# Retention in four chunks of 256 tokens, and the LRU gates' half-empty products in row-group pairs, in a one-core float32 decoder trunk

## The chip, the cores and the metric

One core of a Trainium2 chip (trn2) runs the whole program. The metric is the device time of one execution in microseconds. A product is made of matrix instructions on TensorE (PE in the rows); VectorE is DVE, ScalarE is ACT, GpSimd is POOL, and SyncE (SP) issues the weight DMAs. PEld are the loads of the stationary operand of a matrix instruction.

## What is computed

Two layers on 1024 tokens of width 1024, each a token mixer and a SwiGLU feed-forward. Layer 0 mixes by retention, layer 1 by a gated linear recurrence (RG-LRU). The parts that the change touches:

```python
# retention, 4 heads, dk = 256, dv = 512, state carried over chunks
scores = einsum(q_i, k_i) * intra
o = scores @ v_i + (q_i @ state) * q_decay
state = state * chunk_decay + (k_i * k_decay).T @ v_i
o = rms_norm(o) * silu(g)
# RG-LRU, width 1536, gates are block diagonal: 8 blocks of 192
r = sigmoid(einsum('bsnc,ncd->bsnd', u, w_r) + b_r)
i = sigmoid(einsum('bsnc,ncd->bsnd', u, w_i) + b_i)
a = exp(-8 * softplus(-lam) * r)
b = sqrt(1 - a**2) * (i * u)
h_t = a_t * h_{t-1} + b_t ; y = h * gelu(gate) ; out = y @ w_out
```

The chunk length is free: the sum is the same for any.

## The kernel before

Every product is float32 made of three products of rounded operands (helper `three`, lines 773, 776 and 777: upper by upper, upper by lower, lower by upper), each 128 rows by 128 columns of stationary operand and up to 512 moving columns. An upper part is an ACT or POOL copy, a lower part a DVE or POOL subtraction. PSUM has 8 banks of 512 columns. Jobs that fill a bank are numbered; `psum_full` and `psum_free` count them in order, and `free(e)` lets TensorE wait until job e-8, the earlier user of the bank, is freed.

**Retention.** `head(h)` runs four times. On TensorE: q and k (`tile_rows`), G (the gate, 8 banks), the scores, the turning of k (products with an identity, lines 966 and 967), V (8 banks), then `values(s)` for the eight blocks of 128 tokens, `o_turns` (transposes, line 1009) and the output product. The scores are taken for two chunks of 512 tokens (`CHUNK = 4`): each chunk has key blocks that meet 512, 384, 256 and 128 queries. The state is summed once (`state_sum`, from the first chunk), rounded (ACT line 1500, DVE line 2060), and used by the four blocks of the second. DVE masks the scores (line 2038), splits them (line 2043) and the turned k (line 2048). ACT squares each output block (line 1495) and takes the root (line 1505); DVE gates it (line 2065) and scales it (line 2073). Ahead of that, DVE turns q and k by position (lines 2000 to 2021), first both halves of q, then of k.

**LRU.** The width is cut into four groups of three tiles of 128 (`GT = 3`, items 0 to 5 are three tiles by two halves of 512 tokens). Group by group TensorE does: u (`lru_into(..., 0)`, three times 48 products), the gate branch (`lru_into(..., 6)`), the output product of the group before (`lru_outof`), and then the r and i gates (`lru_gates`). Gate blocks are 192 wide, tiles 128: tile 0 meets rows of tiles 0 and 1, tile 1 those of all three, tile 2 those of 1 and 2 (`MEETS`), so 7 products of three instructions for each of r and i and each half; for the pairs (0, 1) and (2, 1) only 64 of the 128 rows hold anything.

The gate chain follows from the banks: ACT does the sigmoids (lines 1768 and 1773), DVE multiplies u by i and frees two banks (`gated`, line 2392), ACT does tanh, exp and square root (1782, 1786, 1792), each after a load of its function table; DVE does lines 2400 and 2404, the scan (2409) and the gating (2416); ACT rounds y (1800) and DVE splits it (2421). Items go in pairs (0, 1), (2, 3), (4, 5). In DVE's order the next group's convolution (`conv`, lines 2365 and 2367) stands behind the last line 2421 of this group. It reads u's banks, and tile 1 of the next gate branch reuses the first two of them. POOL meanwhile splits the weights of the coming products (touch line 560, cast line 569, subtraction line 571; for the gates' weights 732 and 734).

The last group differs: its gates stand in the midst of the output product of the third. Blocks 0 to 3 come ahead of them, then 4 to 7 (whose banks are those of items 2 and 3), and then the second half (banks of items 4 and 5).

Of the kernel before, what the change touches and what calls it, by code (L numbers as in the profile page):

```python
# [14 lines left out]
P = 128  # L15
D = 1024
S = 1024
# [19 lines left out]
CHUNK = 4  # L37

SCORES = [pieces for c in (0, CHUNK) for pieces in ([(c, 512)], [(c + 3, 128), (c + 1, 384)], [(c + 2, 256)])]
MASK_AT = (P, 0, P)  # L40
SCORE_N = [sum(n for _, n in pieces) for pieces in SCORES]
KT_AT = sum(SCORE_N[:3])
SCORE_AT = [sum(SCORE_N[:i]) + (2 * 512 if i >= 3 else 0) for i in range(len(SCORES))]

KEYS_AT = {c: SCORE_AT[i] + sum(n for _, n in pieces[:j])
           for i, pieces in enumerate(SCORES) for j, (c, _) in enumerate(pieces)}
STATE_AT = sum(SCORE_N) + 2 * 512
SCORE_COLS = STATE_AT + 2 * 512

OT_AT = (0, SCORE_AT[3])  # L50

MEETS = [(0, 1), (0, 1, 2), (1, 2)]
# [4 lines left out]
J_QK, J_G, J_S, J_K, J_V, J_O, J_T, J_W = 0, 8, 16, 22, 24, 32, 40, 48  # L57
# [3 lines left out]
def o_job(s):  # L61

    return J_O + s + (4 if s == SB - 1 else 0)


def t_job(s):
    return J_O + s + (SB - 1 if s < 4 else SB)
# [101 lines left out]
def build(nc, x, positions, mix_norm, ffn_norm, final_norm, ret_w_in, ret_w_out, lru_w_in, lru_conv_w,  # L169
# [3 lines left out]
    with ctx:  # L173
# [79 lines left out]
        def k_turned(d):  # L253

            c = slice(KT_AT + d * 512, KT_AT + (d + 1) * 512)
            return b_hi[:, c], b_lo[:, c]
# [117 lines left out]
        mask_in, k_rounded = sem("mask_in"), sem("k_rounded")  # L374
        st_full, st_rounded, st_ready = sem("st_full"), sem("st_rounded"), sem("st_ready")
# [391 lines left out]
        def _(pe):  # L767
# [164 lines left out]
            def head(h, first, last=False):  # L932
# [11 lines left out]
                for i, pieces in enumerate(SCORES):  # L944
                    if i == 0:
                        pe.wait_ge(qk_ready, h * 8 + 8)
                    free(base + J_S + i)
                    at = 0
                    for c, n in pieces:

                        hf, q = c // CHUNK, c % CHUNK * P
                        for d in range(2):
                            (k_h, k_l), (q_h, q_l) = qk_at(1, d, hf), qk_at(0, d, hf)
                            m = three(bank(J_S + i, at, n), k_h[:, q:q + P], k_l[:, q:q + P],
                                      q_h[:, q:q + n], q_l[:, q:q + n], d == 0, d == 1)
                        at += n
                    m.then_inc(psum_full, 1)
# [3 lines left out]
                for d in range(2):  # L961
                    free(base + J_K + d)
                    k_h, k_l = qk_at(1, d, 0)
                    for c in range(CHUNK):
                        cut, o = slice(c * P, (c + 1) * P), bank(J_K + d, c * P, P)
                        nc.tensor.matmul(o, k_h[:, cut], ident_r[:], start=True, stop=False)
                        m = nc.tensor.matmul(o, k_l[:, cut], ident_r[:], start=False, stop=True)
                    m.then_inc(psum_full, 1)
# [4 lines left out]
                def state_sum():  # L973

                    pe.wait_ge(psum_free, base + J_V + SB)
                    for d in range(2):
                        k_h, k_l = k_turned(d)
                        for c in range(CHUNK):
                            cut, v = slice(c * P, (c + 1) * P), slice(c * 512, (c + 1) * 512)
                            m = three(bank(J_O + 6 + d), k_h[:, cut], k_l[:, cut], a_hi[:, v], a_lo[:, v],  # L980
                                      c == 0, c == CHUNK - 1)
                        m.then_inc(st_full, 1)

                pe.wait_ge(s_ready, h * len(SCORES) + len(SCORES))
                def values(s):
                    late = s >= CHUNK
                    pe.wait_ge(psum_free, base + J_V + s + 1)
                    if s >= 6:

                        pe.wait_ge(st_ready, 2 * h + s - 6 + 1)  # L990
                    for c in range(CHUNK if late else 0, s + 1):
# [3 lines left out]
                                  c % CHUNK == 0, not late and c == s)  # L995
                    for d in range(2 if late else 0):
                        if s == CHUNK:
                            pe.wait_ge(st_ready, 2 * h + d + 1)
                        (q_h, q_l), (st_h, st_l), at = qk_at(0, d, 1), state(d), (s - CHUNK) * P
                        m = three(bank(J_O + s), q_h[:, at:at + P], q_l[:, at:at + P], st_h, st_l, False, d == 1)  # L1000
# [12 lines left out]
                for s in range(3):  # L1013
                    values(s)
                state_sum()
                for s in range(3, SB - 1):
                    values(s)
                o_turns(range(4))
                values(SB - 1)
# [237 lines left out]
            def lru_gates(g, base, e0, u_hi, u_lo):  # L1257

                pe.wait_ge(wri_ready, 2 * g + 2)
                for hf in range(2):  # L1260
                    for tile in range(GT):
                        for m_i in range(2):
                            e = e0 + (hf * GT + tile) * 2 + m_i
                            free(base + e)
                            if m_i == 0 and (hf, tile) in ((0, 0), (0, 1), (1, 1)):

                                pe.wait_ge(u_ready, len(U_PIECES) * g + 2 + tile + hf)
                            for kt in MEETS[tile]:
                                w = slice(m_i * 1152 + kt * 384 + tile * P, m_i * 1152 + kt * 384 + (tile + 1) * P)
                                r = slice(kt * S + hf * 512, kt * S + (hf + 1) * 512)  # L1270
                                m = three(bank(e), wri_hi[:, w], wri_lo[:, w], u_hi[:, r], u_lo[:, r],
                                          kt == MEETS[tile][0], kt == MEETS[tile][-1])
                            m.then_inc(psum_full, 1)

            def lru_outof(g, u0, base, e0, nh, y_hi, y_lo):
                for k in range(GT):
                    j = nh * 3 + k
                    if nh == 0:
                        pe.wait_ge(y_ready, g * 6 + k + 4)
# [18 lines left out]
            for first in (0, 4):  # L1298
                for k in range(GT):
                    if first == 0:  # L1300
                        pe.wait_ge(y_ready, (GROUPS - 2) * 6 + k + 4)
                        pe.wait_ge(w_ready, u0 + 12 + k + 1)
                    w = slice(k * 512, (k + 1) * 512)
                    for s in range(first, first + 4):
                        e = (L_OUT if first == 0 else L_OUT_LAST - 4) + s
                        if k == 0:
# [3 lines left out]
                                  k == 0, k == GT - 1, s == (4 if k else 0))  # L1310
# [10 lines left out]
            def y_there(half, k, i):  # L1321
                if i == 0:
                    pe.wait_ge(y_ready, (GROUPS - 1) * 6 + half * GT + k + 1)
# [12 lines left out]
        def _(act):  # L1336
# [114 lines left out]
            def head(h, first):  # L1451
# [7 lines left out]
                for i in range(8):  # L1459
                    pair, hf, d = i // 4, (i // 2) % 2, i % 2  # L1460
                    act.wait_ge(rope_out, h * 8 + i + 1)
                    nc.scalar.activation(qk_at(pair, d, hf)[0], (t(0), t(1), t(2), r3(7))[i % 4], ACT.Copy)\
                        .then_inc(qk_rounded, 1)
# [7 lines left out]
                for i, n in enumerate(SCORE_N):  # L1471
                    act.wait_ge(psum_free, base + J_S + i + 1)
                    nc.scalar.activation(b_hi[:, SCORE_AT[i]:SCORE_AT[i] + n], T[:, (i % 3) * 512:(i % 3) * 512 + n],
                                         ACT.Copy).then_inc(s_rounded, 1)
                for d in range(2):
                    full(base + J_K + d)
                    nc.scalar.activation(k_turned(d)[0], bank(J_K + d), ACT.Copy).then_inc(k_rounded, 1)
# [5 lines left out]
                act.wait_ge(s_ready, h * len(SCORES) + len(SCORES))  # L1483
# [7 lines left out]
                for s in range(SB):  # L1491
# [5 lines left out]
                    if s == 2:  # L1497
                        for d in range(2):
                            act.wait_ge(st_full, 2 * h + d + 1)
                            nc.scalar.activation(state(d)[0], bank(J_O + 6 + d), ACT.Copy).then_inc(st_rounded, 1)  # L1500
                    if s == 6:
                        o_turned_upper(range(4))
                    if s % 4 == 3:
                        act.wait_ge(o_sq, h * 8 + s + 1)
                        nc.scalar.activation(rstd[:, s - 3:s + 1], ssq[:, s - 3:s + 1], ACT.Sqrt, bias=eps,
                                             scale=1.0 / DV).then_inc(o_root, 1)
                o_turned_upper(range(4, SB))
# [253 lines left out]
            def gate_chain(g, base, e0, y_hi):  # L1761
                def gates(i):

                    tile = i % GT
# [11 lines left out]
                def tanh_exp(items):  # L1776

                    for i in items:
                        if i >= 2:
# [3 lines left out]
                                             scale=gc_gate[:, 21 + i % GT:22 + i % GT]).then_inc(r_tanh, 1)  # L1783
                    for i in items:
                        act.wait_ge(r_tanh, 6 * g + i + 1)
                        nc.scalar.activation(r_buf[i % 4], r_buf[i % 4], ACT.Exp,
                                             scale=gc_gate[:, i % GT:i % GT + 1]).then_inc(a_exp, 1)
# [6 lines left out]
                def y_round(items):  # L1794
                    for i in items:
# [3 lines left out]
                        at = i % GT * S + i // GT * 512  # L1799
# [5 lines left out]
                gates(1)  # L1805
                tanh_exp((0, 1))
                roots((0, 1))
                gates(2)
# [51 lines left out]
        def _(dve):  # L1860
# [130 lines left out]
            def head(h, last=False):  # L1991
                base = JB_RET + h * HEAD_JOBS
                dve.wait_ge(rope_in, h * 32 + 32)
                for pair in range(2):
# [22 lines left out]
                    for i in range(4):  # L2017
# [4 lines left out]
                            .then_inc(qk_ready, 1)  # L2022
                    dve.wait_ge(qk_ready, n + 4)
                dve.wait_ge(rope_saved, 32)
# [5 lines left out]
                for i in range(len(SCORES) + 1):  # L2030
                    if i < len(SCORES):
                        n, m = SCORE_N[i], MASK_AT[i % 3]
                        if i >= 3:
                            dve.wait_ge(s_ready, h * len(SCORES) + i - 2)
                        else:
                            dve.wait_ge(psum_free, base + J_S)
                        full(base + J_S + i)
                        TT(T[:, (i % 3) * 512:(i % 3) * 512 + n], bank(J_S + i, 0, n), dk[:, m:m + n], ALU.mult)\
                            .then_inc(psum_free, 1)
                    if i:  # L2040
                        n, a = SCORE_N[i - 1], SCORE_AT[i - 1]
                        dve.wait_ge(s_rounded, h * len(SCORES) + i)
# [491 lines left out]
```

## Time and profile before

| | us |
|---|---|
| median of 3 runs (2706.28 to 2706.48) | 2706.4 |
| the profiled execution | 2707.8 |
| its span, first to last instruction | 2706.0 |
| TensorE busy | 2673.6 |
| TensorE's loads of the stationary operand | 2213.3 |
| VectorE busy | 1272.0 |
| ScalarE busy | 830.3 |
| GpSimd busy | 1266.6 |

1.8 us of the profiled execution lie outside its span. A row of a timeline gives the start, the duration, engine, line, operation and operands; the next instruction of an engine may start before the duration of the last is over, since they are pipelined: a 512-column instruction lasts 0.39 us, and they start 0.227 us apart. The idle time ahead of an instruction, and who ended it, stands in brackets.

### The profile page before, as it was taken

The page shows a single profiled execution, that of the slowest core. Times are in us where ns is not written, and L with a number is a line of the kernel's source. Part 1 is how long each engine was busy: PE and PEld are TensorE (multiplying, and loading weights), DVE is VectorE, ACT ScalarE, POOL GpSimd, SP SyncE. Part 2 cuts the span into 40 slices and gives each one's busy share as a digit, 9 for nine tenths or more (in the row PEclk, how much of TensorE's full clock was granted, in tenths as well). Part 3 has the DMA queues.
Part 4 walks back from the last instruction along what each step waited for, and adds up shares of the span by engine and source line. Part 5 has one row for each costly group of instructions (what it writes and reads, how often), then busy time and mean ns, then how long its engine had stood idle before and what let it go on. Part 6 is the DMA issues. An engine that isn't in the chain of part 4 may idle for free.

```text
span 2706.0 us, 35201 instructions
## 1 busy us (share of the span) xinstructions
PE 2673.6 (99%) x12017; PEld 2213.3 (82%) x12017; DVE 1272.0 (47%) x1719; ACT 830.3 (31%) x1388; POOL 1266.6 (47%) x1208
## 2 busy tenths in 40 slices
PE   8999999999999999999999999999999999999998
PEld 6888888888888788888888788888887888888887
DVE  8333322323335854444444547365587444444444
ACT  3120120120124533333333515234365222222224
POOL 4323323323423455655555444363454556655555
PEclk9999999999999999999999999999999999999999
DMA  4102102111111111111111021111111111111212
GB/s 142 42 30 63 44 28 63 47 32 59 47 36 43 51 51 54 47 47 54 58 59 54 23 60 44 36 55 39 44 55 47 55 52 49 47 47 54 69 50 83
DMA packets 173768, 139.29 MB, mean 51 GB/s; under 512 B 9200, under 2 KB 143472, under 8 KB 173680
## 3 DMA queue, kind: packets, MB, share of 16 engines
q1 hardware_dynamic: 171584, 133.46, 16.2%
q10 hardware_dynamic: 2096, 4.62, 0.5%
q8 instruction: 59, 0.97, 0.1%
q14 instruction: 29, 0.24, 0.0%
HBM read 132.81 MB, written 5.24 MB: 51 GB/s over the span
## 4 chain that ended last, share of the span: by engine, by line
PE 94%; DVE 3%; ACT 2%; issue 1%; DMA 0%; POOL 0%; SPq 0%; DVEq 0%; ACTq 0%
PE ps L773 31%; PE ps L777 31%; PE ps L776 31%; DVE f_h_lo L2135 1%; ACT gate_buf L1343 0%; PE ps L911 0%; PE ps L1009 0%; PE ps L849 0%; DVE h_sum_a L2124 0%; DVE gate_buf L2209 0%; DMA residual<-in_x 0%; ACT f_h_hi L1581 0%; DVE gate_buf L2073 0%; DVE f_h_lo L2124 0%; ACT f_xn L1625 0%
## 5 line engine op out<-in xcount | busy, mean ns | idle before, releaser
L602 POOL TENSOR_TENSOR f_w_lo<-f_raw,f_w_hi 128x512 fp32r<-128x512 f32 x270 | 357.4, 1325 | 447.8 <-ACT f_w_hi L1532 365.6
L773 PE MATMUL ps<-f_h_hi,f_w_hi 128*128 128x512 f32 x1232 | 481.1, 390 | 4.9 <-DVE f_h_lo L2135 2.1
L777 PE MATMUL ps<-f_h_hi,f_w_lo 128*128 128x512 f32 x1232 | 479.5, 389 | 0.0
L776 PE MATMUL ps<-f_h_lo,f_w_hi 128*128 128x512 f32 x1232 | 479.5, 389 | 0.0
L560 POOL TENSOR_TENSOR small<-w_raw 128x1 f32<-128x1 f32 x200 | 61.0, 305 | 805.2 <-PE ps L773 794.6
L2320 DVE TENSOR_TENSOR residual<-ps,residual 128x512 f32<-128x512 f32 x352 | 239.4, 691 | 171.3 <-PE ps L777 171.3
L773 PEld LDWEIGHTS ps<-f_h_hi,f_w_hi 128*128 128x128 f32 x1232 | 231.2, 188 | 58.9 <-issue 4.3
L1532 ACT ACTIVATE f_w_hi<-f_raw 128x512 fp32r<-128x512 f32 x246 | 154.7, 629 | 383.9 <-PE ps L777 383.8
L777 PEld LDWEIGHTS ps<-f_h_hi,f_w_lo 128*128 128x128 f32 x1232 | 231.2, 188 | 48.2
L776 PEld LDWEIGHTS ps<-f_h_lo,f_w_hi 128*128 128x128 f32 x1232 | 231.3, 188 | 47.2
L773 PE MATMUL ps<-f_w_hi,f_act_hi 128*128 128x512 f32 x688 | 267.9, 389 | 0.6 <-POOL f_w_lo L602 0.6
L776 PE MATMUL ps<-f_w_lo,f_act_hi 128*128 128x512 f32 x688 | 267.7, 389 | 0.0
L777 PE MATMUL ps<-f_w_hi,f_act_lo 128*128 128x512 f32 x688 | 267.6, 389 | 0.0
L571 POOL TENSOR_TENSOR w_lo<-w_raw,w_hi 128x512 fp32r<-128x512 f32 x190 | 258.4, 1360 | 15.2
L773 PE MATMUL ps<-h_hi,w_hi 128*128 128x512 f32 x632 | 247.6, 392 | 0.0
L777 PE MATMUL ps<-h_hi,w_lo 128*128 128x512 f32 x632 | 246.0, 389 | 0.0
L776 PE MATMUL ps<-h_lo,w_hi 128*128 128x512 f32 x632 | 245.9, 389 | 0.0
L602 POOL TENSOR_TENSOR f_w_lo<-f_sum,f_w_hi 128x512 fp32r<-128x512 f32 x124 | 178.7, 1441 | 132.1 <-ACT f_w_hi L1532 124.6
L773 PE MATMUL ps<-w_hi,h_hi 128*128 128x512 f32 x528 | 205.7, 390 | 0.4 <-DVE gate_buf L2012 0.4
L777 PE MATMUL ps<-w_hi,h_lo 128*128 128x512 f32 x528 | 205.5, 389 | 0.0
L776 PE MATMUL ps<-w_lo,h_hi 128*128 128x512 f32 x528 | 205.5, 389 | 0.0
L2275 DVE TENSOR_TENSOR gate_buf<-ps,gate_buf 128x512 f32<-128x512 f32 x120 | 82.8, 690 | 235.1 <-PE ps L777 235.0
(305 smaller groups left out, 4640.8 us busy)
## 6 DMA issues: line engine op xcount, KB each, us to landing
f_raw<-in_ffn_w_gu SPq DMA_DIRECT2D x176, 256.0 KB, 3.3
w_raw<-in_ret_w_in SPq DMA_DIRECT2D x96, 256.0 KB, 2.8
f_raw<-in_ffn_w_down SPq DMA_DIRECT2D x88, 256.0 KB, 2.7
w_raw<-in_lru_w_in SPq DMA_DIRECT2D x48, 256.0 KB, 2.9
w_raw<-in_ret_w_out SPq DMA_DIRECT2D x32, 256.0 KB, 2.6
w_raw<-in_lru_w_out SPq DMA_DIRECT2D x24, 256.0 KB, 2.6
residual<-in_x SPq DMA_DIRECT2D x8, 512.0 KB, 7.7
out_y<-residual SPq DMA_DIRECT2D x7, 512.0 KB, 2.6
```

Source lines behind the costliest of these rows:

```text
L560: nc.gpsimd.tensor_tensor(small[:, 62:63], col, col, ALU.subtract)
L571: nc.gpsimd.tensor_tensor(lo, raw[:, cut], hi.bitcast(F32), ALU.subtract).then_inc(w_ready, 1)
L602: nc.gpsimd.tensor_tensor(lo, src, hi.bitcast(F32), ALU.subtract).then_inc(f_wready, 1)
L773: m = nc.tensor.matmul(o, l_hi, r_hi, start=start, stop=False, skip_group_check=onto)
L776: nc.tensor.matmul(o, l_hi, r_lo, start=False, stop=False, skip_group_check=onto)
L777: return nc.tensor.matmul(o, l_lo, r_hi, start=False, stop=stop, skip_group_check=onto)
L1532: nc.scalar.activation(f_unit(j, last)[0], src, ACT.Copy).then_inc(f_whi, 1)
L2135: TT(H_lo[:, h_cut(form, k)], src[:, t_cut(k)], H_hi[:, h_cut(form, k)].bitcast(F32), ALU.subtract).then_inc(hn_dve, 1)
L2275: TT(t, f_bank(u, p), t, ALU.add).then_inc(f_ev, 1)
L2320: TT(X[:, c], ps[:, b * BANK:(b + 1) * BANK], X[:, c], ALU.add).then_inc(f_ev, 1)
```

## The change

**Retention** goes to four chunks of two blocks (`CHUNK, N_CHUNKS = 2, 4`). The scores of a chunk are one bank: 128 queries for its second key block, 256 for its first. k is turned for three chunks (24 products with the identity instead of 16). The state is summed three times, each time on top of the last in banks 6 and 7 (`onto`), and rounded each time; `values(s)` takes the keys of its own chunk and `from_state(s)` the rest. Since V overwrites q's first half, blocks 2 and 3 of q get a copy of their own (`query_tile`), two more ACT and two more DVE instructions of 256 columns per head in the turning of q. `o_turns` of blocks 0 to 3 now comes ahead of blocks 6 and 7.

**LRU.** The half-empty products are taken with 64 rows, one with rows 0 to 63 and one with rows 64 to 127, alternating (`halves_meet`). The tiles' order is 1, 0, 2; the banks of tiles 0 and 2 are complete only at the end of each half. ACT's sigmoids of item 2 move ahead of the first tanh, DVE's `gated` of item 2 ahead of the scans. In the last group blocks 4 and 5 come before 6 and 7.

```diff
-CHUNK = 4
-SCORES = [pieces for c in (0, CHUNK) for pieces in ([(c, 512)], [(c + 3, 128), (c + 1, 384)], [(c + 2, 256)])]
+CHUNK, N_CHUNKS = 2, 4
+SCORES = [(1, P), (0, 2 * P)]
+SCORE_N = 3 * P
+GATE_TILES = (1, 0, 2)
...
+                for i in range(N_CHUNKS - 1):
+                    free(base + J_K + i)
+                    for d in range(2):
+                        k_h, k_l = qk_at(1, d, i // 2)
+                        for c in range(CHUNK):
+                            q = (i % 2 * CHUNK + c) * P
+                            cut, o = slice(q, q + P), bank(J_K + i, (d * CHUNK + c) * P, P)
+                            nc.tensor.matmul(o, k_h[:, cut], ident_r[:], start=True, stop=False)
+                            m = nc.tensor.matmul(o, k_l[:, cut], ident_r[:], start=False, stop=True)
...
-                for s in range(3):
-                    values(s)
-                state_sum()
-                for s in range(3, SB - 1):
-                    values(s)
-                o_turns(range(4))
-                values(SB - 1)
+                values(0)
+                values(1)
+                state_sum(0)
+                for i in (1, 2):
+                    values(2 * i)
+                    values(2 * i + 1)
+                    from_state(2 * i)
+                    from_state(2 * i + 1)
+                    state_sum(i)
+                o_turns(range(4))
+                for s in (6, 7):
+                    values(s)
+                    from_state(s)
...
+                    def halves_meet():
+                        for m_i in range(2):
+                            a_w, a_wl, a_u, a_ul = operands(0, m_i, 1, slice(0, 64))
+                            b_w, b_wl, b_u, b_ul = operands(2, m_i, 1, slice(64, P))
+                            a, b = bank(event(0, m_i)), bank(event(2, m_i))
+                            nc.tensor.matmul(a, a_w, a_u, start=False, stop=False)
+                            nc.tensor.matmul(b, b_w, b_u, start=False, stop=False)
+                            nc.tensor.matmul(a, a_w, a_ul, start=False, stop=False)
+                            nc.tensor.matmul(b, b_w, b_ul, start=False, stop=False)
+                            nc.tensor.matmul(a, a_wl, a_u, start=False, stop=True)
+                            m = nc.tensor.matmul(b, b_wl, b_u, start=False, stop=True)
+                        m.then_inc(psum_full, 4)
+                    if hf == 0:
+                        pe.wait_ge(u_ready, len(U_PIECES) * g + 2)
+                    meets(0, 0, True, False)
+                    meets(1, 0, True, False)
+                    meets(1, 1, False, False)
+                    pe.wait_ge(u_ready, len(U_PIECES) * g + 3 + hf)
+                    meets(1, 2, False, True)
+                    meets(2, 2, True, False)
+                    halves_meet()
...
-            for first in (0, 4):
+            for first, n in ((0, 4), (4, 2), (6, 2)):
...
+                    if pair == 0 and hf == 0:
+                        nc.scalar.activation(query_tile(d)[0], src[:, 256:512], ACT.Copy).then_inc(q2_rounded, 1)
...
                 gates(0)
                 gates(1)
+
+                gates(2)
                 tanh_exp((0, 1))
                 roots((0, 1))
-                gates(2)
                 gates(3)
...
-                gated((0, 1))
-
-                scans((0, 1), amid=lambda: gated((2,)))
+                gated((0, 1, 2))
+                scans((0, 1))
                 gated((3,))
```

## Rows read from the trace of the kernel before

**Rows 1.** The page: busy time of the engines, and the chain that ended last

```profile
PE 2673.6 (99%) x12017; PEld 2213.3 (82%) x12017; DVE 1272.0 (47%) x1719; ACT 830.3 (31%) x1388; POOL 1266.6 (47%) x1208
PE 94%; DVE 3%; ACT 2%; issue 1%; DMA 0%; POOL 0%; SPq 0%; DVEq 0%; ACTq 0%
```

**Rows 2.** Waits of TensorE (line waiting, releaser: us in total, times, longest)

```profile
PE ps L911 <- DVE xn L1886: 2.9, 1, 2.9
```

**Rows 3.** Timeline of TensorE, scores and turning of k, head 1

```profile
322.93 0.39 PE L773 MATMUL ps<-a_hi 128*128 128x512 f32 x1
...
324.29 0.22 PE L773 MATMUL ps<-a_hi 128*128 128x128 f32 x1
...
324.91 0.39 PE L773 MATMUL ps<-a_hi 128*128 128x384 f32 x1
...
326.02 0.28 PE L773 MATMUL ps<-a_hi 128*128 128x256 f32 x1
...
326.74 0.39 PE L773 MATMUL ps<-q_late_hi,a_hi 128*128 128x512 f32 x1
...
330.56 0.22 PE L966 MATMUL ps<-ident_r,a_hi 128*128 128x128 f32 x1
...
332.30 0.44 PE L773 MATMUL ps<-w_hi,h_hi 128*128 128x512 f32 x1
```

**Rows 4.** Timeline of DVE, end of V and the state, head 1

```profile
372.14 5.44 DVE L2053 SCALAR_TENSOR_TENSOR a_lo<-ps,gam,a_hi 128x512 fp32r<-128x512 f32 x8 [38.21 <-ACT a_hi L1481]
...
386.26 0.69 DVE L2060 TENSOR_TENSOR b_lo<-ps,b_hi 128x512 fp32r<-128x512 f32 x1 [2.03 <-ACT b_hi L1500]
```

**Rows 5.** Timeline: turning of k by position, heads 0 and 1; DVE on 256 columns

```profile
71.67 0.50 PE L773 MATMUL ps<-w_hi,h_hi 128*128 128x512 f32 x1 [0.35 <-DVE gate_buf L2012]
...
268.73 0.69 DVE L2000 TENSOR_TENSOR tmp<-ps,gate_buf 128x512 f32<-128x512 f32 x1 [1.43 <-PE ps L777]
...
327.43 0.42 DVE L2038 TENSOR_TENSOR tmp<-ps,mask 128x256 f32<-128x256 f32 x1
```

**Rows 6.** TensorE in the gates of the last group (us, busy, instructions, clock, DMA)

```profile
1948.90:1967.90 19.00, 19.00 (x85) 1.00 0.00 1
```

**Rows 7.** Timeline of ACT, DVE and TensorE: gate chain of the last group

```profile
1956.50 0.71 ACT L1782 ACTIVATE gate_buf<-tmp,gc_gate 128x512 f32<-128x512 f32 x1
...
1968.98 0.69 DVE L2392 TENSOR_TENSOR uc<-uc,tmp 128x512 f32<-128x512 f32 x1
...
1969.72 0.50 PE L773 MATMUL ps<-w_hi,a_hi 128*128 128x512 f32 x1 [0.25 <-DVE uc L2392]
```

**Rows 8.** Timeline: group 1's gates begin; first convolutions, and TensorE where it needs them

```profile
1677.85 3.98 DVE L2367 SCALAR_TENSOR_TENSOR uc<-ps,gc_conv,uc 128x1023 f32<-128x1023 f32 x3
...
1685.08 0.39 PE L773 MATMUL ps<-h_hi,w_hi 128*128 128x512 f32 x1
...
1739.48 0.39 PE L773 MATMUL ps<-a_hi,wri_hi 128*128 128x512 f32 x1
...
1747.66 0.74 ACT L1782 ACTIVATE gate_buf<-tmp,gc_gate 128x512 f32<-128x512 f32 x1
...
1796.64 3.98 DVE L2367 SCALAR_TENSOR_TENSOR uc<-ps,gc_conv,uc 128x1023 f32<-128x1023 f32 x3
```

**Rows 9.** Timeline of DVE and POOL, groups 0 and 1

```profile
1643.18 1.29 DVE L2421 TENSOR_TENSOR a_lo<-gate_buf,a_hi 128x512 fp32r<-128x512 f32 x2
...
1759.05 3.06 POOL L560 TENSOR_TENSOR small<-w_raw 128x1 f32<-128x1 f32 x1 [22.44 <-PE ps L773]
...
1778.80 4.55 DVE L2421 TENSOR_TENSOR a_lo<-gate_buf,a_hi 128x512 fp32r<-128x512 f32 x2 [2.15 <-ACT a_hi L1800]
...
1779.80 2.99 POOL L734 TENSOR_TENSOR wri_lo<-wri_raw,wri_hi 128x1152 fp32r<-128x1152 f32 x1
```

**Rows 10.** The critical chain in order of time: transposes at the LRU's start

```profile
1546.62 6.02 PE ps L911 x24
1554.23 0.87 PE ps L911 x8
```

## What bounds the kernel, what the change does to it, and the forecast

> **What bounds the kernel.** I read the page first. TensorE is busy 2673.6 of 2706.0 us and 94% of the chain that ended last is TensorE's [rows 1], so an instruction taken from it counts in full, unless something that was hidden comes out. So TensorE's waits come next: few and short. Two matter here. 2.9 us stand at the LRU's start [rows 2], and 0.25 us once on the gate chain's DVE line 2392 [rows 7]. Then the timeline, stage by stage, for the slack of ACT, DVE and POOL wherever TensorE will now come sooner. One slot of a 512-column instruction is 0.227 us: the 84 of one group's gates take 19.0 us [rows 6].
>
> **Retention, TensorE's work.** In head 1 the scores run from 322.93 to 330.56, 7.63 us for two chunks; the turning of k ends at 332.30, 1.74 us for 16 products [rows 3]. Six 512-column products are 1.36 us, but six of 128 columns 0.62 (324.29 to 324.91), not a quarter: they start 0.11 apart, as do the turnings. Six of 256 are 0.72 (326.02 to 326.74) [rows 3]. A chunk of two blocks is one set of each, 1.34 us, four are 5.36. 24 turnings are 1.5 x 1.74 = 2.61. Together 7.97 against 9.37: 1.40 less a head, 5.6 in four. `values`, state and `from_state` are 108 slots before (84 + 24) and after (72 + 36), and the transposes only move: nothing. Should a 128-column set not profit from the wider product ahead of it (its first gap is 0.06 instead of 0.11), the scores cost 0.2 more a head: 4.8 to 5.6.
>
> **Retention, new waits.** The first state sum waits for all of V. DVE's line 2053 ends at 377.58 [rows 4], 1.67 us after V's last product (375.91 by the count of slots); ahead of the sum now stand nine slots, 2.04 us, instead of 18. Slack 0.4, cost 0; if it is gone, at most 0.4 a head. Each state goes through ACT and DVE: in the only case before, DVE's second half ended at 386.95 [rows 4], 1.5 us after the sum (ended 385.45 by slots). `from_state` comes nine slots later (2.04 us) and its second half 0.68 after that; ACT's two squares and its root, which stand ahead of the rounding, finish within the 2.72 us of the state sum. Cost 0. Ahead of block 6 stand 16 transposes (16 x 0.109 = 1.75 us, rate of [rows 10]) and one product: 0 too. On ACT the squares, on DVE `gate_o`, are queued behind the roundings; DVE had stood idle 2.0 us ahead of that row. Turning of q: two more DVE instructions of 256 columns, 0.42 each and some 0.34 apart [rows 5], 0.7 in all. In head 1 DVE waits 1.43 us for TensorE afterwards, in heads 2 and 3 alike; in head 0 it doesn't, and TensorE waited for its line 2012 there [rows 5]: +0.7. Retention in sum: -5.6 + 0.7 = **-4.9** (-4.1 to -5.6).
>
> **LRU gates, TensorE's work.** A half has 42 slots; now 30, and 12 half-empty products. Bounds for these: 12 slots, 2.72 us, if they run one after another, and 1.33 if two at a time and only the loads' 0.11 us count. Nothing in the trace runs on 64 rows. I take 1.6, near the lower end, since a pair needs two loads, 0.22, which just fit a slot, and add two changes of 0.1 for going in and out. Half: 8.4 instead of 9.52; the gates 16.8 instead of 19.0, 2.2 less a group.
> The Trainium skill ("TensorE: Matmul & The Clock Gate", Part 3, Measured speedup vs the span model) gives 3.07 times for four row tiles; an estimate from that is 1.77 us. "TensorEngine Tiling (Array Packing)", Tiling Modes, says that changing the tiling mode drains the engine. No run here shows either yet.
>
> **LRU, what is late next.** The gate chain can't start on item 1 before the half is complete, and six sigmoids (0.58 apart) precede the first tanh. In groups 0 and 3 it began 7.6 us after the gates (1956.50 against 1948.9) [rows 6, 7]. Now: 8.4 + 0.2 + 4 x 0.58 + 0.1 = 11.0, +3.4. DVE saves `gated` of item 2 between the scans, 0.6: chain +2.8. In groups 1 and 2 DVE's additions held it until 8.2 (1747.66 against 1739.48) [rows 8]: +2.2.
> In DVE's queue the next group's convolution stands behind this chain, and TensorE's second gate-branch tile waits for its first tile (two banks). That tile begins 19.04 + 192 slots = 62.6 us after the gates' start (1685.08 less 1622.5), and the convolution is done at 59.3 in group 0 (1681.83) and 61.1 in group 1 (1800.62 less 1739.48) [rows 8]; group 2 is like 1. So slack is 3.3, 1.4, 1.4, and the change takes 2.2 + 2.8 or 2.2 + 2.2 from it.
> Against that: DVE's instructions with two SBUF inputs and POOL's take turns. Line 2421 takes 1.29 us for two in group 0 but 4.55 in group 1, where POOL's line 734, 2.99 us long, fell on it [rows 9]. Shifted by 4 us they miss each other, and line 734 meets scans and gating that are half covered by ACT: of 3.3 I take back 1.9, so that in groups 1 and 2 the convolution ends at 61.1 + 2.2 - 1.9 = 61.4, and in group 0 at 59.3 + 2.8 = 62.1. TensorE gets there at 60.4 and waits 1.7, 1.0, 1.0. Gains: 0.5, 1.2, 1.2, less 0.3 for the banks of tile 0, needed 2.7 us sooner at the gates' start, where DVE's additions free them: **-2.6**.
>
> **LRU, the last group.** Gates end at 16.8, blocks 4 and 5 are 18 slots, to 20.9. Blocks 6 and 7 need item 3. DVE freed it at 1969.6 (line 2392 [rows 7]), 20.7 after the start, and TensorE lost 0.4 in sum on it. Now 20.7 + 2.8 = 23.5: a wait of 2.6, then 18 slots: 27.7, where it was 27.7 before (19.04 + 8.16 + 0.4). The gates' gain is lost here. Besides, POOL may split the next weights only when k = 1 of blocks 6 and 7 has begun, 1.4 + 0.65 after 23.6; cast and subtraction take 2.1 to 2.4: +0.3. The chain's +2.8 also reaches DVE's steps before the second feed-forward, for which I put +0.7, an estimate between nothing (slack eats it) and 2.5 (it comes through nearly whole). Sum **+1.0**.
>
> **Sum.** -4.9 - 2.6 + 1.0 = -6.5. Against the profiled execution's own 2707.8 (span 2706.0 and 1.8 around it) that is 2701.3; the median, 1.4 lower, gives **2699.9**, and 2700 is my forecast.
>
> **Rivals.**
> 1. POOL falls on the first scans. The first weight split after the gates (cast and subtraction, 1.9 us; begins 17.5 after the gates' start) used to come when DVE was nearly through with items 0 and 1, and POOL waited 3.06 us for DVE [rows 9]. Now it falls into lines 2400 and 2404 of these items. If DVE yields there as it did later (4.55), the chain loses some 2 there and 2 more in the shifted rest, and the convolution ends at 65: waits of 4.7 instead of 1 to 1.7, -2.5 per group against before, 2706.4 - 4.9 + 7.5 + 1 = 2710. It ends slower if TensorE's clock falls too: at the LRU's start it went to half after a wait of 2.9 us, and 24 transposes took 6.02 us where 8 take 0.87 later [rows 2, 10], 3.4 us lost. Three times: 2720. It decides from a convolution that ends later than 63. For it: both engines are fuller than before in that stretch. Against: POOL was held off in both groups.
> The Trainium skill ("SBUF — State Buffer", Summary: rules for kernel authors) says that with two SBUF inputs on DVE the second to issue blocks until the first finishes; by that rule, rival 1.
> 2. The halves run one after another: the gates stay at 19.04, the chain is 1.1 later still, the three groups gain nothing (+0.5 in sum), the last loses 1.5 more. 2706.4 - 4.9 + 0.5 + 2.5 = 2704.5. For it: the change is only in which rows are read; no row shows two at once.
> 3. The chain is covered everywhere: 3 x 2.2: 2706.4 - 4.9 - 6.7 + 1 = 2696. Against: slack is 1.4 in two groups.
> 4. The forecast, but the last group's wait of 2.6 halves the clock: +3.4, 2703.4. The wait is near the 2.9 that did [rows 2].
>
> **Chances.** Forecast 0.39; rival 1 0.17 (a third of it with the clock); 2 0.12; 3 0.12; 4 0.20. 0.2% is 5.4 us, about what a measurement of this kernel tells from no change: faster is below 2701.0, slower above 2711.8. Faster: 0.31 of the forecast's 0.39, rival 3, and 0.05 of the others: 0.48. Slower: 0.13. Same: 0.39. The range reaches from rival 3 with its bound to rival 1 between its two ends: 2695 to 2714.
>
> **What would show it.** Scores and turnings at 8.0 us a head. In `halves_meet` two products starting within one slot, a half in 8.4. ACT's first tanh 11 after the gates' start. TensorE waiting for line 2367 in the second gate-branch tile of groups 1 to 3 (1 to 2 us; 5 in rival 1), and for line 2392 in the last group by some 2.5. The clock row beside it. Wrong would make it: products on 64 rows starting 0.23 apart, a wait before the first state sum, or no wait at 2367.

## The result, and the profile after

The changed kernel takes 2715.9 us (median of 8, 2712.8 to 2717.9) against 2706.4 (2706.1 to 2707.4): ratio 1.0034, interval 1.0025 to 1.0043. It is 9.5 us slower. The forecast was 2700.0, 2695 to 2714; the sign was wrong and the time lies 1.9 above the range. The profiled execution took 2716.6, its span is 2714.8, 8.8 more than before's.

The page of the changed kernel, busy time and the chain that ended last:

```profile
PE 2670.7 (98%) x12049; PEld 2205.4 (81%) x12049; DVE 1290.2 (48%) x1731; ACT 839.9 (31%) x1408; POOL 1265.4 (47%) x1208
PE 86%; DVE 8%; ACT 4%; issue 2%; DMA 0%; POOL 0%; DVEq 0%; SPq 0%; ACTq 0%
```

TensorE is busy 2.9 us less than before, while the span is 8.8 longer, and DVE has risen from 3 to 8% of the chain [rows 1]. The busy time hides part of the loss, since an instruction at half clock also counts as busy. TensorE's waits from the LRU's start to the second feed-forward's (waiting line, releaser: us in total, times, longest), where before there were the one at the LRU's start [rows 2] and 0.25 us in the last group [rows 7]:

```profile
PE ps L792 <- DVE uc L2443: 10.8, 3, 3.7
...
PE ps L930 <- DVE xn L1955: 2.9, 1, 2.9
...
PE ps L792 <- DVE uc L2469: 2.1, 1, 2.1
```

Three waits for the first tile of a convolution (2443 is the line 2367 of before), one for the gating of item 3 in the last group (2469, before 2392 [rows 7]). The granted clock in the stretch behind each of these four (us, busy of PE, PEld, DVE, ACT and POOL, clock, DMA share, GB/s):

```profile
1680.90:1686.90 6.00, 6.00 (x15) 4.75 (x16) 5.83 (x5) 0.00 (x0) 2.02 (x3) 0.54 0.14 45
1802.80:1808.80 6.00, 5.99 (x20) 4.81 (x21) 5.82 (x5) 0.00 (x0) 2.02 (x3) 0.74 0.14 44
1923.40:1929.40 6.00, 6.00 (x15) 4.75 (x16) 5.82 (x5) 0.00 (x0) 2.02 (x3) 0.55 0.15 44
1979.50:1985.50 6.00, 5.99 (x19) 4.77 (x20) 4.39 (x7) 5.97 (x10) 2.74 (x6) 0.72 0.01 1
```

In 6 us TensorE began 15 to 20 instructions, where 26 fit at one slot each: the clock was at 1.2 instead of 2.4 GHz for part of each stretch. The 60 instructions behind the waits took 2.7, 1.6, 2.7 and 1.8 us longer than 60 slots. At the full clock such a stretch takes 0.1 longer (full_rows, below), so nearly all of the first three is the clock. Of the last 1.8 not all is: in hold (below), behind the same wait and at the full clock, the same 60 took 0.6 longer.

Where the 8.8 us are, by the starts of the same product in both traces: the start of the program, before anything that was changed, -0.8 (no effect of the change); the four heads -4.7; the 75 us from the LRU's first transposes to the first gates -0.7, with the clock there low for a shorter time (0.72 over the first 6 us, before 0.50); from each of the first three groups' gates to the next +4.8, +3.8, +4.6; the last group and all that follows +1.7. The three groups are 3 x -1.84 (gates) + 11.3 (waits, start to start less one slot) + 7.0 (clock) + 0.5 (not placed) = 13.3.

### The profile page after: what moved, and what is told of

The parts are those of the page before. It is cut to its first block, busy times and chain, and to the rows that moved or that the text cites. A ratio compares the mean times of both kernels' runs of the same rounds, so it can differ in the third digit from the quotient of the medians.

```text
span 2714.8 us, 35330 instructions
## 1 busy us (share of the span) xinstructions
PE 2670.7 (98%) x12049; PEld 2205.4 (81%) x12049; DVE 1290.2 (48%) x1731; ACT 839.9 (31%) x1408; POOL 1265.4 (47%) x1208
## 4 chain that ended last, share of the span: by engine, by line
PE 86%; DVE 8%; ACT 4%; issue 2%; DMA 0%; POOL 0%; DVEq 0%; SPq 0%; ACTq 0%
PE ps L792 28%; PE ps L795 28%; PE ps L796 28%; DVE uc L2486 1%; DVE f_h_lo L2211 1%; DVE gate_buf L2491 1%; DVE a_lo L2496 0%; DVE uc L2443 0%; ACT gate_buf L1407 0%; PE ps L1039 0%; DVE scratch L1988 0%; ACT L1860 0%; ACT L1853 0%; DVE h_sum_a L2200 0%; ACT xn L1839 0%
## 5 line engine op out<-in xcount | busy, mean ns | idle before, releaser
L579 POOL TENSOR_TENSOR small<-w_raw 128x1 f32<-128x1 f32 x200 | 52.5, 263 | 815.8 <-PE ps L792 806.2
```

The costliest lines, as they stand in the source:

```text
L579: nc.gpsimd.tensor_tensor(small[:, 62:63], col, col, ALU.subtract)
```

## The experiments

Each was timed beside the kernel before, which took 2706.55 beside ret_only, lru_only, conv_first and wri_later, 2706.59 beside both, best, late_sig and full_rows, 2706.56 beside hold, probe and both_full, 2706.24 beside all3. Times are medians; what is read from a trace is of one execution. "Stretched" means below: by how much the 36 DVE instructions of a group's chain are longer in sum than undisturbed ones (0.69 us each, a scan 1.22).

**The two parts, each alone.** ret_only is the kernel before with the retention part; lru_only has only the LRU part.

> The retention part of the change alone, with the LRU as in the kernel before. By the prediction's sum for retention it is 4.9 us faster than before (4.1 to 5.6): 2701.5. The two traces at hand say 4.7 from the end of k's and q's first products to the LRU's start (1510.3 against 1505.6). A rival, that the larger number of states and turnings costs something hidden by the LRU's waits later, would give less than 3 us.

> The LRU part of the change alone, with the retention of the kernel before. If the two parts only add up, it is 13 to 15 us slower than before (2720): four gates 1.8 us shorter each, three waits of 3.8 us for line 2367's first tile with 1.5 to 2.8 us lost to the clock behind each, and a wait of 2.2 with 1.7 lost in the last group. A rival, that part of the loss comes from retention's end shifting against the weight splits, would give clearly less than 13.

ret_only: 2701.9, -4.7 (ratio 0.9984, 0.9975 to 0.9993). lru_only: 2720.4, +13.8 (1.0054, 1.0040 to 1.0068). Sum +9.1 against the 9.5 measured: the parts add up, and all that was lost was lost in the LRU.

**Taking the convolution out of the late queue.** conv_first only changes DVE's order: the last two lower parts of y (line 2496) come behind the first tile of the next convolution.

```diff
+                    if tile == 0:
+                        behind_first()
...
-                y_split((4, 5))
+                if whole:
+                    y_split(g, y_hi, y_lo, (4, 5))
...
-                conv(g, base, 0)
+                conv(g, base, 0, lambda: y_split(g - 1, a_hi, a_lo, (4, 5)))
```

> The changed kernel, but DVE takes a group's last two lower parts of y behind the first tile of the next convolution instead of ahead of it. Theory A (TensorE waits because DVE's queue reaches the convolution late, and the clock falls because of the wait's length): the convolution's first tile ends 2.8 us sooner in each of three groups, the waits are 1.0 instead of 3.8, the clock stays whole behind them, 2716 - 3 x 2.8 - 7 = 2700.6. Theory B (the clock falls for another reason, such as the change of row groups in the gates): only the waits shorten, 2707.6, and the clock still falls three times.

2701.7 (2701.3 to 2702.1), 14.3 less than the changed kernel. Waits of TensorE, and the clock behind the first of them:

```profile
PE ps L792 <- DVE uc L2443: 2.3, 3, 0.9
```

```profile
1677.00:1686.00 9.00, 8.27 (x37) 6.79 (x37) 8.79 (x9) 2.31 (x2) 4.33 (x6) 1.00 0.10 30
```

Moving two instructions that take 2.8 us returned 8.5 us of waits and the clock of all three places (1.00 in each). The 64-row products are still there, so they alone don't lower the clock: theory A.

**Moving POOL's large split.** wri_later has `gates(g, 2 * g, 0)`, the split of half of the next gates' weights, on POOL behind the first three units of the next six (a unit is one weight tile of 128 x 512 that POOL splits).

> The changed kernel, but POOL splits the first half of the next gates' weights (lines 751 and 753) three units later, past the chain's gating and lower parts. Theory A (half of the chain's delay is POOL's subtraction of 3.5 us falling on DVE's lines 2491 and 2496): the chain ends some 3 us sooner, waits of about 1 us, no half clock behind them: about 2700. Theory C (POOL's other splits, which were queued behind it, move up and take the same time from DVE): the waits stay at 3 us or more, 2713 to 2716.

2706.3 (2704.4 to 2707.4), between the two. Two groups now wait 0.8 and 1.0 us, one 3.8, and behind that one the clock fell again (2.5 us). DVE and POOL ahead of it:

```profile
1787.79 2.23 DVE L2497 TENSOR_TENSOR a_lo<-gate_buf,a_hi 128x512 fp32r<-128x512 f32 x2
1789.95 2.64 DVE L2429 COPY gc_conv<-cols 128x24 f32 x1
1792.74 1.34 DVE L2442 TENSOR_SCALAR uc<-ps,gc_conv 128x1024 f32<-128x1024 f32 x1 [0.15 <-DVE gc_conv L2429]
```

```profile
1789.56 2.99 POOL L753 TENSOR_TENSOR wri_lo<-wri_raw,wri_hi 128x1152 fp32r<-128x1152 f32 x1
```

The chain was stretched 7 to 8 us instead of 13, but in this group the moved subtraction fell on a copy of 24 columns per partition that stands ahead of the convolution: 2.64 us, against 1.12 in this kernel's other two groups and 0.17 in all three of the changed kernel. Both theories have a share: without the split in it the chain is shorter, and in this group the split took a part of its price along to where it was moved.

**Both edits.** both joins them; all3 adds the edit of hold, below.

> The convolution's first tile ahead of the last lower parts, and POOL's split of the first half of the gates' weights three units later, in one kernel. Theory A: the waits for the convolution, 0.8 to 1.1 with the first edit alone, go to 0.3 or less; with the first edit's 2701.7 that gives 2699.4. Theory C (POOL's other splits move up into the chain, as the 3.8 us that one group still waited with the second edit alone suggest): a wait of 1 us or more stays in at least one group, 2700.5 to 2702.

> All three remedies in one: POOL's first split held until the second scan is done, the convolution's first tile ahead of the last lower parts, and the split of the first half of the gates' weights three units later. With the last two alone there was no wait for the convolution left (2698.2), so theory A gives no more gain: 2698.2, within 0.5. If POOL, held once, hands the weights over too late, TensorE waits for POOL in the units behind the gates: 2699 or more.

both: 2698.2 (2697.9 to 2698.4; ratio 0.9969, 0.9957 to 0.9980), no wait for the convolution. all3: 2698.4. Nothing more is to be had there. both is the version that beats the kernel before, by 8.3 us, and the changed one, by 17.7.

**Holding POOL's first split back.** In the prediction this was rival 1. POOL waits until DVE's second scan is done before it splits the first unit behind the gates:

```diff
-                units(6, u0, now)
+                units(2, u0, now)
+                pool.wait_ge(l_scan, 6 * g - 4)
+                units(6, u0, now, first=2)
```

> The changed kernel, but POOL starts the first weight split after the gates only when DVE's second scan is done (23 us after the gates' start instead of 17.7). Theory A (that split costs the chain the 1.5 us by which lines 2481 and 2486 of items 0 and 1 are stretched): the waits for the convolution are 2.3 instead of 3.8, 2716 - 4.5 = 2711.5, less up to 7 more if the clock then stays whole. Theory C (the split falls on the next DVE instructions and takes the same there): 2714 to 2717.

2699.2 (2698.6 to 2700.7), 16.7 less than the changed kernel by adding a wait to it, and 5 below the lowest that theory A allowed. Group 1's first items in the changed kernel, DVE and then POOL (start, duration):

```profile
1755.75 0.68 DVE L2477 SCALAR_TENSOR_TENSOR tmp<-gate_buf,tmp 128x512 f32<-128x512 f32 x1
1756.35 0.69 DVE L2481 TENSOR_TENSOR uc<-uc,gate_buf 128x512 f32<-128x512 f32 x1
1756.95 1.10 DVE L2481 TENSOR_TENSOR uc<-uc,tmp 128x512 f32<-128x512 f32 x1
1757.98 2.31 DVE L2486 TENSOR_TENSOR_SCAN uc<-tmp,uc 128x512 f32<-128x512 f32 x1
```

```profile
1755.94 0.55 POOL L579 TENSOR_TENSOR small<-w_raw 128x1 f32<-128x1 f32 x1 [20.78 <-PE ps L792]
1756.43 1.08 POOL L588 CAST w_hi<-w_raw 128x512 fp32r<-128x512 f32 x1
1757.59 1.62 POOL L590 TENSOR_TENSOR w_lo<-w_raw,w_hi 128x512 fp32r<-128x512 f32 x1
1761.40 0.65 POOL L579 TENSOR_TENSOR small<-w_raw 128x1 f32<-128x1 f32 x1 [2.19 <-PE ps L792]
```

and with POOL held:

```profile
1751.19 0.68 DVE L2483 TENSOR_TENSOR uc<-uc,tmp 128x512 f32<-128x512 f32 x1
1751.79 1.22 DVE L2488 TENSOR_TENSOR_SCAN uc<-tmp,uc 128x512 f32<-128x512 f32 x1
...
1754.04 1.27 DVE L2493 TENSOR_TENSOR gate_buf<-uc,gate_buf 128x512 f32<-128x512 f32 x2
1755.23 0.69 DVE L2471 TENSOR_TENSOR uc<-uc,tmp 128x512 f32<-128x512 f32 x1
1755.83 1.29 DVE L2498 TENSOR_TENSOR a_lo<-gate_buf,a_hi 128x512 fp32r<-128x512 f32 x2
```

```profile
1754.35 2.82 POOL L579 TENSOR_TENSOR small<-w_raw 128x1 f32<-128x1 f32 x1 [24.99 <-DVE uc L2488]
```

In the changed kernel POOL's touch of one column comes 0.8 us after DVE's run began (1755.14), goes through in 0.55 us, and the cast and subtraction behind it stretch DVE's product to 1.10 and its scan to 2.31. Held back, the same touch arrives in the midst of DVE's back-to-back gating and is kept out for 2.82 us, through five DVE instructions of undisturbed length; so it was in the kernel before, 3.06 us [rows 9]. From the first tanh to the end of the convolution's first tile pass 50.3 us in this group (1743.3 to 1793.6) against 53.6 (1749.1 to 1802.7), and the chain is stretched 9.4 instead of 13.3 (before 10.2). The later splits fall more kindly too, which the expectation left out. Of the waits for the convolution 0.6 us in sum are left.

The Trainium skill ("SBUF — State Buffer", SBUF: two separate sides) calls the access that the two engines share an exclusive lock, which a DVE instruction with two SBUF inputs, or the GpSimd one, holds to its end if it starts first. The stretched scan (2.31) agrees with that in kind. The 2.82 us go beyond it: POOL stayed out over five DVE instructions, and not over one.

What decides which engine yields is not shown. It isn't the place in DVE's run alone: in the changed kernel the next touch (1761.40) falls into the same run, 6.3 us after its start and on the same gating that keeps POOL out in hold, and takes 0.65, though there POOL had been at work in that run before.

**The pairs.** full_rows is the changed kernel with the half-empty products over all 128 rows; both_full is the same in the kernel with both edits.

```diff
-                            a_w, a_wl, a_u, a_ul = operands(0, m_i, 1, slice(0, 64))
-                            b_w, b_wl, b_u, b_ul = operands(2, m_i, 1, slice(64, P))
+                            a_w, a_wl, a_u, a_ul = operands(0, m_i, 1)
+                            b_w, b_wl, b_u, b_ul = operands(2, m_i, 1)
```

> The changed kernel with its order and sigmoids, but the half-empty products over all 128 rows, so no two run at once. Each half is 42 slots, 9.5 instead of 8.6 us, the first tanh 0.9 later. The convolution is 0.9 later after the gates' start and TensorE's second gate-branch tile 1.8 later, so its wait is 0.9 shorter (2.9): +0.9 in each of three groups, +1.8 - 0.9 in the last: 2716 + 3.7 = 2719.7 while the clock still falls; theory B (the 64-row products cause the falls): no falls, 2711.

> The kernel with both edits (2698.2, no waits for the convolution), but the half-empty products over all 128 rows. There the pairs' worth is not hidden: each gate is 19.0 instead of 17.2 us, +1.84 in three groups, and +1.84 less the 0.7 to 0.9 by which the last group's wait shrinks: +6.5, 2704.7. If the pairs are worth nothing even there, 2698.2.

full_rows: 2709.7 (2708.8 to 2710.3), 10 less than I expected; both_full: 2704.5, as expected. So the pairs are worth 6.3 us where nothing waits, and in the changed kernel they cost 6.2. The waits of full_rows for the convolution, and the clock behind the longest:

```profile
PE ps L792 <- DVE uc L2443: 4.2, 3, 1.9
```

```profile
1800.70:1806.70 6.00, 5.97 (x26) 4.96 (x27) 5.83 (x5) 0.52 (x1) 2.03 (x3) 1.00 0.13 44
```

1.4 us each instead of 3.6, and the clock whole in every one. The gates, 1.84 longer, bring TensorE later to the tile that waits; and though the first tanh is 1.1 later after the gates' start (12.1 against 11.0 in group 1), the convolution's first tile ends no later (64.6 in both), since POOL's splits fall otherwise again (the chain is stretched 11.5). The full clock is no proof for theory B: conv_first and both have the pairs and keep it. My error here was to hold the stretch and the clock fixed.

**The third item's sigmoids.** late_sig puts them behind the first roots again, and DVE's gating of item 2 between the scans.

> The changed kernel, but the third item's sigmoids stand behind the first roots again, and DVE multiplies it between the scans, as in the kernel before; pairs and tile order stay. The first tanh comes 1.15 us sooner, DVE's first gating 0.6 sooner. If chain and waits move one for one, the three waits are 3.2 instead of 3.8 and still halve the clock: 2714. Rival (the collisions with POOL sit differently and decide more than the shift): off by 2 us or more to either side.

2712.8 (2710.9 to 2715.5), near the 2714 but not by its reasoning:

```profile
PE ps L792 <- DVE uc L2469: 11.7, 4, 3.0
```

No wait for the convolution is left; instead TensorE waits 2.9 us on average in all four groups for item 2's banks right behind the gates, and the clock fell behind three of them. The gates are now too short for the old order: the early sigmoids are what the pairs need, not an extra.

**Item 3 between the scans.** best is both, with DVE's gating of item 3 between the first two scans.

> As the kernel with both edits, and DVE multiplies item 3 by its gate between the first two scans instead of behind the gating of y. The last group's wait of 2.1 us should go to 0.7, 1.4 less, and where its clock fell (1.7 us) it should no longer fall; the chain of items 0 and 1 is 0.6 later at its gating, while item 3's product is only moved. Forecast 2697 (2696 to 2698.5). Rival: the chain's end sets what follows, and the gain of 1.4 comes back as a wait ahead of the second feed-forward: 2699.

2701.1 (2699.3 to 2703.1), 2.8 more than both. Waits of TensorE in it:

```profile
PE ps L793 <- DVE residual L2059: 4.4, 2, 2.9
...
PE ps L793 <- DVE uc L2479: 1.5, 1, 1.5
```

The wait of 2.1 is gone, but one of 1.5 stands where the product's second half begins, for the banks of item 4, and 19.5 us later TensorE waits 2.9 for DVE's additions, which stand in DVE's queue behind the first instructions (line 2400 of before) of items 4 and 5. The rival was right in kind: in the last group what isn't waited for here is waited for further on. The trace is of one of the fastest executions (2699.4), 0.9 above that of both, and its clock stays whole behind both waits; the rest of the 2.8 us is in none of the traces, though the three executions above 2702.4 have a lower mean clock (0.997) than those below 2700 (0.998 and 0.999).

**What a wait costs.** probe is conv_first with DVE instructions of 512 columns that nobody reads ahead of the convolution, three in groups 1 and 2, two in group 3.

> The kernel with the convolution's first tile ahead of the last lower parts (2701.7, waits of 0.9, 1.1 and 0.8, no fall of the clock behind them), and DVE instructions of 512 columns that nobody reads ahead of the convolution: three in groups 1 and 2, two in group 3, some 0.6 us each. The waits should be 2.7, 2.9 and 2.0. If only their length costs, 2701.7 + 1.8 + 1.8 + 1.2 = 2706.5. If a wait of 2.7 or more halves the clock and one of 2.0 doesn't (the wait of 2.1 in the kernel with whole rows did not), 1.6 to 2.8 more each for two: 2710 to 2712. Theory B (the clock falls because of what the gates do) says 2706.5.

2711.3 (2709.0 to 2713.0). Its waits for the convolution, and the clock behind each:

```profile
PE ps L792 <- DVE uc L2445: 7.7, 3, 2.9
```

```profile
1680.20:1686.20 6.00, 6.00 (x14) 4.74 (x15) 5.82 (x6) 1.03 (x1) 2.02 (x3) 0.50 0.15 45
1801.50:1807.50 6.00, 5.97 (x19) 4.80 (x20) 5.82 (x6) 1.02 (x1) 2.31 (x3) 0.72 0.14 44
1920.70:1926.70 6.00, 5.96 (x19) 4.74 (x20) 5.82 (x6) 2.31 (x2) 2.38 (x3) 0.72 0.16 44
```

5.4 us of added waits cost 9.6 by the medians, and 11.6 in the two traced executions (2713.0, probe's slowest, against 2701.4). The 60 instructions behind the waits took 2.9, 1.7 and 1.8 us longer than 60 slots: with the same gates, longer waits alone bring the clock down. The third wait, of 1.9, did so too, which the expectation did not have; the same wait in full_rows had not.

## Why the prediction was wrong, step by step

- **Retention, TensorE's work: right.** Head 1 of the changed kernel, scores, turning and what follows:

```profile
321.47 0.22 PE L792 MATMUL ps<-a_hi 128*128 128x128 f32 x1
...
326.99 0.22 PE L987 MATMUL ps<-ident_r,a_hi 128*128 128x128 f32 x1
...
329.62 0.45 PE L792 MATMUL ps<-w_hi,h_hi 128*128 128x512 f32 x1
```

  The scores take 5.52 (forecast 5.36), the turning 2.63 (2.61): 8.15 against the 9.37 of before [rows 3], and later heads are 1.3 to 1.5 us shorter as a whole, against 1.40.
- **Retention, new waits: right.** None ahead of the state sums. Head 0's turning of q: DVE's two waits there are 0.3 and 0.4; up to its turning of k the head gained 1.5 where its scores alone gain 2.1, so 0.6 went to q (forecast 0.7). In sum -4.7, by ret_only and by the trace, against -4.9.
- **Gates, TensorE's work: right in kind, 0.36 short.** The pairs run two at a time:

```profile
1623.21 0.49 PE L1320 MATMUL ps<-a_hi,wri_hi 64*128 64x512 f32 x1
1623.22 0.49 PE L1321 MATMUL ps<-a_hi,wri_hi 64*128 64x512 f32 x1
1623.55 0.39 PE L1322 MATMUL ps<-a_lo,wri_hi 64*128 64x512 f32 x1
...
1624.81 0.50 PE L792 MATMUL ps<-a_hi,wri_hi 128*128 128x512 f32 x1
```

  From the first pair to the next full product pass 1.60 us, the value taken. But of the four gaps that are 0.1 longer than a slot (before and behind the first pair, before and behind the first full product) two lie outside it, so a half takes 8.6, not 8.4, and the gates 17.2: -1.84, not -2.2. Rival 2 is refuted. The Trainium skill ("TensorEngine Tiling (Array Packing)", Tiling Modes) says that a change of tiling mode drains the engine; the trace agrees: the first such gap is 0.31 where a slot is 0.227.
- **The first tanh: right.** In group 0 it begins at 1627.2, the gates at 1616.3: 10.9, forecast 11.0.
- **"Of 3.3 I take back 1.9": the step that failed.** It said that the chain, shifted by 4 us, and POOL's large split would miss each other. They met:

```profile
1778.85 3.70 DVE L2491 TENSOR_TENSOR gate_buf<-uc,gate_buf 128x512 f32<-128x512 f32 x2
1782.64 2.62 DVE L2496 TENSOR_TENSOR a_lo<-gate_buf,a_hi 128x512 fp32r<-128x512 f32 x2
```

```profile
1777.93 3.47 POOL L753 TENSOR_TENSOR wri_lo<-wri_raw,wri_hi 128x1152 fp32r<-128x1152 f32 x1
```

  Two gatings at 3.70 instead of 1.27. The chain was stretched 13.3 to 13.6 us in every group, where it had been 8.5, 10.2 and 10.2: it rose by 3 to 5 us where the prediction had it fall by 1.9, and in group 0, where it had it stay, too. The convolution's first tile ended 64.4 to 64.6 us after the gates' start, where the prediction had 62.1, 61.4 and 61.4, and each wait was 3.6 instead of 1.7, 1.0 and 1.0: +7.1 on the sum.
- **Rival 1 was that mechanism**, with the convolution at 65 and waits of 4.7. Its place was right (POOL's first split on the first scans). "Against: POOL was held off in both groups" was true of the old timing alone: with the new one the same touch went through in 0.55 us, and in hold, 5 us into DVE's run, it was held off again. It had a chance of 0.17, and with the clock a third of that.
- **The clock: priced too high for one case, and left out of the forecast.** Waits of 1.0 to 1.7 may well have kept it: behind those of 0.6 to 0.9 in conv_first and of 1.1 to 1.9 in full_rows it stayed whole. With 3.6 it fell each time, for 1.6 to 2.7 us, not 3.4. That is 7.0 us in the groups. Rival 1 with the clock (2720) is the case that came, some 4 us milder.
- **The last group: the wait right, the rest not.** TensorE waited 2.1 us (2.2 start to start; forecast 2.6), and the 60 instructions behind it took 1.8 longer, as in rival 4. Gates -1.8, wait +1.8, clock and weights +1.6, sum +1.7 with all the rest. The +0.3 for the weights is covered here by the slow clock; hold, at the full clock, has it (its first product behind blocks 6 and 7 starts 0.3 late, held by POOL's subtraction). The +0.7 for what follows didn't show.
- **The sum.** -4.7 - 5.5 + 11.3 + 7.0 + 0.5 - 0.7 + 1.7 = +9.6, and the medians say +9.5.

## What to carry to other kernels

When a product gets shorter, redo the slack of every other engine's queue behind it: here DVE, which POOL's instructions stretch, had 1.4 us left in two groups, and the saving of 1.84 turned into a wait of 3.6 plus a slow clock; moving two instructions that nobody was waiting for (conv_first) gave 14.3 us back, and one added wait on POOL (hold) 16.7. A collision between two engines is no constant that moves along with a shift: lay the two queues side by side at their new times, and bound the sum by both cases, the one engine held off and the other stretched. And a wait of 2 us or more ahead of TensorE can have two prices: the wait, and the half clock behind it, which the busy time hides.

## What the runs showed of the hardware that was not expected

- A one-column POOL instruction was kept out for 2.8 to 3.1 us by a run of DVE instructions (hold, and before), but took 0.55 us when it came 0.8 us after the run's start (the changed kernel); then DVE's instructions were stretched instead, a scan from 1.22 to 2.31. Nor is it always kept out in the midst of a run: 0.65 us at 6.3 us into one (the changed kernel), and 1.21 us at 4.7 us into another, on its scans, in the kernel before:

```profile
1982.64 1.21 POOL L560 TENSOR_TENSOR small<-w_raw 128x1 f32<-128x1 f32 x1 [2.84 <-PE ps L773]
```

  What decides it stays open.
- A copy of 24 columns on DVE took 2.64 us beside POOL's subtraction of 2.99 (wri_later), and 0.17 in the changed kernel.
- The length of a wait doesn't settle whether the clock halves behind it. From the LRU's first gates on, with waits of 3.4 us and more it fell 7 times of 7 (after, lru_only, wri_later). With 2.8 to 3.0 it fell 5 times of 7: not in best, nor in group 0 of late_sig, where the first row is that group and the second the next:

```profile
1637.00:1643.00 6.00, 6.00 (x27) 4.94 (x27) 5.63 (x8) 4.60 (x8) 5.50 (x4) 1.00 0.01 3
1755.50:1761.50 6.00, 6.00 (x21) 4.79 (x21) 5.76 (x8) 4.68 (x8) 5.28 (x3) 0.75 0.00 0
```

  The last group's wait of 2.1 behind identical work halved it in four kernels (after, conv_first, both, probe) and not in four others (lru_only, wri_later, hold, all3). This lot, four times in one execution, is also the likely reason why the changed kernel's runs spread over 5.1 us where before's spread over 1.4: its fastest run has a mean clock of 0.997, its slowest of 0.995. It was not tested by itself.
- The wait of 2.9 at the LRU's start was followed by half clock in all 14 kernels, for a longer time in the kernel before [rows 10] and in both_full (0.50 and 0.51 over the first 6 us) than in the other twelve (0.72). What decides between the two at a given length stays open.
